# Late tiles' weights through the merge's buffers, the samples' expert sums slot by slot, and the last prompt slots shared with TensorE

## The reference, cut to what matters

```
branch A, B, M -> merged = sum_c sigmoid(xn @ w_gate[c]) * (o_c @ w_branch[c])     (1024 channels)
h = x + merged @ w_out                         # linear "out"
xf = rmsnorm(h); q = xf @ w_pq                 # norm "ffn", linear "pq"
idx, g = top 16 experts per head, 8 heads      # 128 experts per token
a = gelu(u_tab[idx] . xf)
y = h + sum_k g_k * a_k * v_tab[idx_k]
```

## Time and profile before

| | us |
|---|---|
| median of 3 runs | 2679.56 (2672.99 to 2693.68) |
| profiled execution, its own time | 2691.42 |
| its span in the trace | 2689.7 |
| DVE busy | 1760.5 (65%) |
| PE busy | 1799.8 (67%) |
| gathers and other POOL DMAs (queue q0) | 577.16 MB of 727.63 MB |

### The profile page before, as it was taken

The page is one execution under the profiler, slowest core; times in us unless marked ns, Lnnn a source line. Parts: engine busy times, 40 slices in busy tenths (PEclk is TensorE's granted clock), DMA queues, the critical chain, the costliest instruction groups (busy, mean ns, idle before and its releaser), DMA issues.

```text
span 2689.7 us, 25069 instructions
## 1 busy us (share of the span) xinstructions
PE 1799.8 (67%) x6605; PEld 989.1 (37%) x6605; DVE 1760.5 (65%) x3916; ACT 671.3 (25%) x2036; POOL 867.9 (32%) x829
## 2 busy tenths in 40 slices
PE   7999889699845747782458748577755552965312
PEld 3467466454422312231222217355533322551010
DVE  3353465621147796667769988888646886785886
ACT  2010266420113322332213322222222121321221
POOL 1000043210004642233325435322334775332350
PEclk9999889899978988896779985688887565557756
DMA  5121230033409889889799889989988999989985
GB/s 144 35 92 63 70 139 2 1 126 141 148 4 413 349 352 375 342 354 393 298 385 384 319 322 391 351 324 349 335 325 310 347 383 413 364 344 390 380 357 207
DMA packets 200776, 727.63 MB, mean 271 GB/s; under 512 B 39769, under 2 KB 83186, under 8 KB 133754
## 3 DMA queue, kind: packets, MB, share of 16 engines
q0 software_dynamic: 84384, 577.16, 53.8%
q1 hardware_dynamic: 114442, 144.25, 15.8%
q10 hardware_dynamic: 1808, 4.61, 0.5%
HBM read 717.36 MB, written 12.66 MB: 271 GB/s over the span
## 4 chain that ended last, share of the span: by engine, by line
issue 10%; DMA 10%; DVE 10%; PE 9%; SPq 9%; POOL 3%; DVEq 1%; ACT 0%; ACTq 0%; POOLq 0%
SPq L1321 4%; SPq L1320 4%; DVE heads_t L3335 3%; DMA branch_rows_t<-in_uv_tab,e_idx 3%; PE sl_at_l_ps L1985 1%; DMA heads_t<-in_uv_tab,e_idx 1%; PE fq_pq_acc L490 1%; DVE branch_rows_t L3340 1%; DMA fq_out_w<-in_w_out 1%; DMA is_ch<-in_cache_a_kidx,chunk_rows 1%; PE ex_y_ps L3402 1%; PE sl_at_ps L2029 1%; DMA ex_pairs<-in_uv_tab,e_idx 1%; DMA fq_pq_w<-in_w_pq 1%; PE sl_at_kt_ps L1980 1%
## 5 line engine op out<-in xcount | busy, mean ns | idle before, releaser
L3308 POOL DMA_INDIRECT ex_pairs<-in_uv_tab,e_idx x147 | 191.2, 1301 | 574.9 <-issue 275.9
L3368 ACT ACTIVATE ex_coef<-ex_dots 128x1 f32<-128x1 f32 x512 | 103.6, 202 | 1047.2 <-DVE ex_dots L3340 983.5
L3308 POOL DMA_INDIRECT branch_rows_t<-in_uv_tab,e_idx x163 | 191.1, 1172 | 309.5 <-DVE heads_t L3335 178.2
L3308 POOL DMA_INDIRECT heads_t<-in_uv_tab,e_idx x146 | 183.4, 1256 | 251.0 <-DVE heads_t L3335 135.6
L3340 DVE CUSTOM_DVE_ANT_0 branch_rows_t<-branch_rows_t,heads_t 128x1024 f32<-128x1024 f32 x163 | 198.9, 1220 | 41.0 <-DMA branch_rows_t<-in_uv_tab,e_idx 39.3
L3340 DVE CUSTOM_DVE_ANT_0 ex_pairs<-ex_pairs,heads_t 128x1024 f32<-128x1024 f32 x147 | 179.7, 1223 | 62.8 <-DMA ex_pairs<-in_uv_tab,e_idx 60.3
L824 PE MATMUL in_acc<-in_w,xn_t 128*128 128x512 f32 (+7 forms) x560 | 207.8, 527 | 6.4 <-POOLq L183 4.3
L3340 DVE CUSTOM_DVE_ANT_0 heads_t<-heads_t 128x1024 f32<-128x1024 f32 x146 | 178.3, 1222 | 47.6 <-DMA heads_t<-in_uv_tab,e_idx 44.2
L3335 DVE SCALAR_TENSOR_TENSOR heads_t<-branch_rows_t,ex_coef,heads_t 128x1024 f32<-128x1024 f32 x118 | 151.3, 1283 | 38.7 <-issue 26.5
L1346 PE MATMUL cs_pp<-cs_ch,xn_t 128*128 128x256 f32 x512 | 132.3, 423 | 54.6 <-DMA cs_ch<-in_cache_cmp_kv 54.6
L3370 ACT ACTIVATE ex_coef<-ex_coef,e_gate 128x1 f32<-128x1 f32 x512 | 150.8, 295 | 16.6
(11 more groups left out here) (738 smaller groups left out, 3440.5 us busy)
## 6 DMA issues: line engine op xcount, KB each, us to landing
cs_ch<-in_cache_cmp_kv SPq DMA_DIRECT2D x256, 128.0 KB
fq_mg_wg<-in_w_gate SPq DMA_DIRECT2D x6, 2048.0 KB, 26.3
in_w<-in_w_in SPq DMA_DIRECT2D x4, 2048.0 KB, 11.6
first_w<-in_w_gate SPq DMA_DIRECT2D x3, 2048.0 KB, 8.2
fp_wb<-in_w_branch SPq DMA_DIRECT2D x6, 1024.0 KB, 10.2
fp_wg<-in_w_gate SPq DMA_DIRECT2D x3, 2048.0 KB, 7.9
fq_mg_wb<-in_w_branch SPq DMA_DIRECT2D x6, 1024.0 KB, 29.4
fs_blocks<-in_w_branch SPq DMA_DIRECT2D x6, 1024.0 KB, 19.1
```

What stands on the lines that cost most here:

```text
L3308: pool.indirect_dma_start(out=pair(s), out_offset=None, in_=i["uv_tab"], in_offset=bass.IndirectOffsetOnAxis(ap=idx[:, t, m:m + 1], axis=0 ...
L3368: act.activation(c, dots[:, t, m:m + 1], ACT.Gelu_apprx_tanh).then_inc(gelu_done, 1)
```

## The change

There are four edits:

1. `fq` now takes its merge buffers from `finish_rows`, as the early tiles did. SP loads the first half of w_out into wg0 when the matmuls of merge job 4 are done, the second half into wg1 and the first half of w_pq into wb when those of job 5 are; the second half of w_pq goes to wg0 when the first half of out has been multiplied. The norm puts its squares and its gain into wg1.
2. `merge_samples` has the stored gates loaded by ACT, not by SP behind the blocks.
3. `adds_on_vector` leaves every second slot from n = 482 on to PE (15 of the last 30 slots).
4. `expert_samples` makes gelu, gate product, diagonal and matmuls for each of the 8 slots as soon as its dot is there, all of the first three on ACT.

```diff
+SAMPLE_ROWS = 485
...
-    return not beside_search or m % 2 == 0
+    return not beside_search and step < SAMPLE_ROWS or m % 2 == 0
...
@@ finish_rows
-            if early:
-                wg = [self.first_w[:], self.sb(f"{tag}_wg", [P, KD, 512], F32, tmp)[:]]
+            if not last:
+                sem = self.sem if early else self.gather_sem
+                wg = [self.first_w[:], self.sb(f"{tag}_wg", [P, KD, 512], F32, tmp)[:]] if early else [
+                    self.sb(f"{tag}_wg{n}", [P, KD, 512], F32, tmp)[:] for n in range(2)]
                 wb = self.sb(f"{tag}_wb", [P, 2, 4, 512], F32, tmp)
                 weights = (wg, wb)
-                out_w = (wg, [self.sem(f"{tag}_out_in{b}") for b in range(2)])
-                pq_w = ([wb[:].rearrange("p a k n -> p (a k) n"), wg[0]], [self.sem(f"{tag}_pq_in{b}") for b in range(2)])
+                out_w = (wg, [sem(f"{tag}_out_in{b}") for b in range(2)])
+                pq_w = ([wb[:].rearrange("p a k n -> p (a k) n"), wg[0]], [sem(f"{tag}_pq_in{b}") for b in range(2)])
...
             space = None
+            if late:
+                words = wg[1].rearrange("p k n -> p (k n)")
+                space = h, xf, words[:, :D], words[:, D:2 * D], self.sb(f"{tag}_ffn_ss", [P, nt], F32, tmp)
...
@@ merge_samples, the program of SP
-                    sp.wait_ge(*remembered)
-                    sp.dma_start(gate8, self.s["gate8"].rearrange("j b n -> b j n")).then_inc(gate_in, 16)
...
+                @block.scalar
+                def _(act):
+                    act.wait_ge(*remembered)
+                    act.dma_start(gate8, self.s["gate8"].rearrange("j b n -> b j n")).then_inc(gate_in, 16)
...
@@ expert_samples, PE
-                        yield at(MIXED + 2 + 0.3 * n)
+                        yield at(MIXED + 1.2 - 0.9 * (N - n))
                         pe.wait_ge(diag_done, n + 1)
...
@@ expert_samples, ACT
-                    yield at(MIXED + 0.5)
-                    act.wait_ge(dot_done, N)
-                    act.activation(coef[:], dots[:], ACT.Gelu_apprx_tanh).then_inc(gelu_done, 1)
-                    yield at(MIXED + 1)
-                    act.wait_ge(coef_done, 1)
                     for n in range(N):
-                        yield at(MIXED + 1.1 + 0.3 * n)
-                        act.activation(diag[:, n, :], same[:], ACT.Copy, scale=coef[:, n:n + 1]).then_inc(diag_done, 1)
+                        yield at(MIXED + 0.9 - 0.9 * (N - n))
+                        one = coef[:, n:n + 1]
+                        act.wait_ge(dot_done, n + 1)
+                        act.activation(one, dots[:, n:n + 1], ACT.Gelu_apprx_tanh).then_inc(gelu_done, 1)
...
+                        act.activation(one, one, ACT.Copy, scale=gate[:, n:n + 1]).then_inc(coef_done, 1)
+                        act.wait_ge(coef_done, n + 1)
+                        act.activation(diag[:, n, :], same[:], ACT.Copy, scale=one).then_inc(diag_done, 1)
```

More of the change, by code:

```diff
@@ L2797, in finish_rows @@
             else:
-                self.merge(tag, x_t, o_t, rows, mixed, also, weights=weights, after=after, samples=not early)
+                self.merge(tag, x_t, o_t, rows, mixed, also, weights=weights, after=after, samples=not early, first_here=early)
             load_h = None
@@ L2896, in finish, with merge @@
         self.expert_samples(h[:, 0], xf[:DB, 0, :], keys, self.iota32[:, :PTOP])
-    def merge(self, tag, xT, oT, rows, mixed, also, weights=None, after=(), samples=False):
+    def merge(self, tag, xT, oT, rows, mixed, also, weights=None, after=(), samples=False, first_here=False):
         nc, i = self.nc, self.i
@@ L2932, in _ @@
                                 store(j - depth)
-                        if j or not weights:
+                        if j or not first_here:
                             sp.dma_start(wg[j % depth], i["w_gate"][:, D * c + 512 * q:D * c + 512 * q + 512].rearrange("(k p) n -> p k n", p=P)).then_inc(w_in[j % depth], 16)
@@ L2954, in _ @@
                         if t == 0:
-                            if weights and j == 0:
+                            if first_here and j == 0:
                                 pe.wait_ge(self.first_w_in, 16)
                             else:
-                                pe.wait_ge(w_in[j % depth], 32 * (j // depth + 1) - (16 if weights and j % depth == 0 else 0))
+                                pe.wait_ge(w_in[j % depth], 32 * (j // depth + 1) - (16 if first_here and j % depth == 0 else 0))
                         if samples and t == 0:
@@ L2969, in _ @@
                         last.then_inc(gate_mm, 1)
-                        if weights and u == 0:
+                        if first_here and u == 0:
                             pe.wait_ge(w_in[0], 16)
@@ L3448, in expert_samples @@
             stored = self.stores("y_sample")
-            (zeroed, q_done, same_done, scored, score_out, spread, x_out, chain, idx_done, top_done, exp_done, dot_done, gelu_done, coef_done, diag_done,
+            (zeroed, q_done, same_done, scored, score_out, spread, x_out, chain, idx_done, top_done, exp_done, gate_done, dot_done, gelu_done, coef_done, diag_done,
              mix_done, y_done) = (self.sem(f"es_{n}") for n in (
-                 "zeroed", "q", "same", "scored", "score_out", "spread", "x_out", "chain", "idx", "top", "exp", "dot", "gelu", "coef", "diag",
+                 "zeroed", "q", "same", "scored", "score_out", "spread", "x_out", "chain", "idx", "top", "exp", "gate", "dot", "gelu", "coef", "diag",
                  "mix", "y"))
@@ L3502, in _ @@
                     act.activation(fv[:], fv[:], ACT.Exp, bias=top[:], accum_out=total[:]).then_inc(exp_done, 1)
-                    yield at(MIXED + 0.5)
-                    act.wait_ge(dot_done, N)
-                    act.activation(coef[:], dots[:], ACT.Gelu_apprx_tanh).then_inc(gelu_done, 1)
-                    yield at(MIXED + 1)
-                    act.wait_ge(coef_done, 1)
-                    for n in range(N):
-                        yield at(MIXED + 1.1 + 0.3 * n)
-                        act.activation(diag[:, n, :], same[:], ACT.Copy, scale=coef[:, n:n + 1]).then_inc(diag_done, 1)
+                    for n in range(N):
+                        yield at(MIXED + 0.9 - 0.9 * (N - n))
+                        one = coef[:, n:n + 1]
+                        act.wait_ge(dot_done, n + 1)
+                        act.activation(one, dots[:, n:n + 1], ACT.Gelu_apprx_tanh).then_inc(gelu_done, 1)
+                        if n == 0:
+                            act.wait_ge(gate_done, 2)
+                        act.wait_ge(gelu_done, n + 1)
+                        act.activation(one, one, ACT.Copy, scale=gate[:, n:n + 1]).then_inc(coef_done, 1)
+                        act.wait_ge(coef_done, n + 1)
+                        act.activation(diag[:, n, :], same[:], ACT.Copy, scale=one).then_inc(diag_done, 1)
                     yield 1.0
@@ L3513, in _ @@
                     act.dma_start(self.o["y_sample"][:, 0, :], y[:DB, :]).then_inc(stored, 16)
+                    yield 2.0
                     act.wait_ge(stored, 16)
@@ L3573, in _ @@
                     for rows, cols in halves:
-                        c.link(dve.tensor_scalar(gate[rows, :], fv[rows, cols], total[rows, 0:1], None, ALU.mult))
+                        dve.tensor_scalar(gate[rows, :], fv[rows, cols], total[rows, 0:1], None, ALU.mult).then_inc(gate_done, 1)
                     for n in range(N):
@@ L3581, in _ @@
                                                  accum_out=dots[:, n:n + 1]).then_inc(dot_done, 1)
-                    yield at(MIXED + 0.7)
-                    dve.wait_ge(gelu_done, 1)
-                    dve.tensor_tensor(coef[:], coef[:], gate[:], ALU.mult).then_inc(coef_done, 1)
                     yield 1.0
```

## The result

The changed kernel takes **2649.65 us** (median of 4 runs, 2648.74 to 2652.02) against 2679.22 us of the kernel before (median of 4, 2672.99 to 2693.68): a ratio of 0.9877, interval 0.9851 to 0.9902. That is 29.6 us less; forecast were 35 less and 2645. All medians and ratios in this document leave out the one execution of the kernel samples_at_end that took 3746 us, 41% above the seven others of that kernel.

What follows compares the result with a forecast made beforehand. The prediction took DMA to bound the kernel, with DVE close behind. Its terms, -14 (edit 1), -1 (edit 2) and -20 (edits 3 and 4), sum to -35 from 2679.6: 2644.6 us, 8-in-10 range 2626 to 2672.

Steps and rivals of the forecast that it cites:

- Edit 1, the added wait: Stage fq: ACT's gate8 waits for a store queued behind weight loads, delaying DVE's gate product by 26.4 us.
- Edit 1, the waits removed: Stage fq: DVE's waits at the out add, at pq and for displaced gathers go, together -43.9 us.
- upper end: Edit 1's worst case: store lands at 1266 after 47.7 us, DVE's product 67 us late, +11 to +23 us.
- The last gather: End of the kernel: the last gather starts 3.8 us earlier.
- the five sums: Five fewer DVE sums before the samples' indices are ready, bringing the first es gather up by 6 us.
- The last dot: End: four of eight DVE-bound steps behind the last gather lose their sum, 4 x 1.2 = -4.8 us.
- Behind the last dot: End: fewer samples' matmuls remain, so the y add comes at T + 7 instead of T + 18.5, -11.5 us.
- T: The time the last dot is over: about 2664.4 before, forecast 2655.7.
- cold PE: Rival at the end: PE stays at half clock, edits 3 and 4 bring only -3, time 2662; chance 0.12.
- No hazard at the store: Rival in stage fq: gate8's store lands within a few us or ACT gets by; edit 1 -28, time 2631; 0.12.
- the late store: Rival in stage fq: gathers crowd SP's queue, store lands between 1240 and 1262, time 2655 to 2670; chance 0.15.
- The end brings nothing: Rival: last gather doesn't move, T stays; -11 instead of -20, time 2653; chance 0.03 given together with another case.

Runs made afterwards that it cites:

- samples_at_end: Changed kernel without edit 4: the samples' gelu, product, diagonals and matmuls all behind the last es dot; 2657.40 us (median of 7), ratio 0.9926 to the kernel before.
- h_unwaited: Changed kernel with gate8 stores ahead of the weights, w_pq's first half behind fq_h, and DVE waiting for fq_h only at the out add; 2633.93 us, ratio 0.9807.
- only_ahead: Kernel before with edit 1 alone, without edits 2, 3 and 4; 2668.12 us, ratio 0.9953 to the kernel before.
- no_alternation: Changed kernel without edit 3, so DVE adds all of the last slots; 2656.23 us, ratio 0.9890 to the kernel before.

## Why the prediction was right, point by point

- **What bounds.** That time saved is worth what the DMA engines leave idle decided edit 2 (0 us of a 25 us wait) and kept edit 1 at 11 us. In h_unwaited the DMA share of stage fq reaches 0.97, near its end.
- **Edit 1, the added wait.** Forecast +26.4; slots 110 to 120 took 57.7 for 31.1, **+26.6**, and 57.4 to 57.8 in all seven traces whose stores stand behind the weights. The store went out at 1207.05, which is 1218.4 on the time axis of before, when the last matmuls of the merge were done (forecast 1218), and landed 12.4 us later (forecast 14). ACT idled 35.05 us, not the 25 that the prediction's last paragraph asks for: it came to gate8 10 us before DVE ran out of work.
- **Edit 1, the waits removed.** Forecast -43.9; slots 120 to 170 took 141.8 for 179.5, **-37.7**. Here the sum was 6 us too good. It had all of DVE's waits for gathers in this stretch gone, 4.1, 1 and 6.3 us; they fell from 11.7 to 7.7 us, at a DMA share of 1.00. Net -11.1, forecast -14, which had allowed for some of it (-12.6 by the ratio of only_ahead). One sum of the upper end is wrong as it stands: a landing at 1266 would put DVE's product near 1268 by the prediction's own 1.5 us for ACT, 61 us late and not 67.
- **Edit 2.** Forecast -1, measured +0.3 between slots 440 and 480. I had said that waits for gathers would take its place; what showed up was a wait for PE and a longer one for the norm's gain. Any of them can hold the place, since behind them the same bytes have to pass.
- **The last gather.** Forecast 3.8 us earlier, near the 3.6 us of idle transfer time and not the 6 us of the five sums (the prediction doesn't say where the 0.2 comes from). POOL's last gather moved by 25.1 us, slot 480 by 21.3: **-3.8**. The first es gather, forecast 6 us earlier, moved by 3.7 beyond slot 480.
- **The last dot.** Forecast -4.8 more, measured -3.6 more: slots 480 to 511 gained 7.4 of 8.6.
- **Behind the last dot.** Forecast y add at T + 7, measured T + 5.2, and 6.2 to the end for 6.8: -13.8 for -11.5.
- **PE's clock.** The rival of a cold PE didn't come. PE was at 0.50 in front of the samples' matmuls and had 1.00 from 2620 on, after groups that followed each other without a gap from 2614.49 on. The Trainium skill, "TensorE: Matmul & The Clock Gate", section "HAM oscillation — how this bites in real kernels", has a kernel whose groups of matmuls are shorter than the waits for DMA between them, and each group starts cold. This trace agrees for the prompt slots ahead of 2614: behind gaps of 6.76 and 8.60 us they took 3.78 us at a clock of 0.50. The samples' groups aren't a case of it, since there are no waits between them. Nor does no_alternation put it to the test, where the groups took 1.88 us with gaps of only 1.60 between, at a granted clock of 1.00 from 2626 to 2646 (PE's timeline of that kernel):

```profile
2626.58 1.88 PE L3497 MATMUL es_y_ps<-es_pairs,es_diag 128*8 128x512 f32 x4 [1.60 <-ACT es_diag L3522]
```

  So the prediction, which had taken any wait between groups for such a case, took the rule for wider than the page has it.
- **Rivals.** "No hazard at the store" fell by ACT's 35.05 us; the late store didn't come: no gather was asked for while DVE stood (POOL idled 32.54 us up to 1225.83). That this is why it landed early was not tested. "The end brings nothing" fell by the 7.4 us of slots 480 to 511.
- **The sum.** Forecast -35; by the terms of the trace -31.3, by medians -29.6. Edit 1 gave 2.9 less, slots 170 to 480 2.1 less and the last slots 1.2 less than forecast, the end 2.3 more. So the total is nearer to the forecast than its terms are: the end's surplus, which is luck, makes up for a part of what the others lack.

What I didn't see: that behind the store fq_h stands in the same queue. With the store out of the way slots 120 to 130 take 19.9 us more, and most of that is transfer time that has to be spent in any case: with fq_h no longer waited for, the stage gains another 6.6 us and not 19.9.
